# Loading the first memory head's cached keys inside the last differential head, both key products ahead of the sample scores, and memory queries made as 1, 2, 1 and 0 per head

## The chip, the cores and the metric

The kernel runs on one core of one Trainium2 chip. The core has a matrix engine (TensorE, PE in the profile; PEld is its weight load), a vector engine (VectorE, DVE), an activation engine (ScalarE, ACT), a general engine (GpSimd, POOL) and a queue engine (SyncE, SP) that issues nearly all transfers; 16 DMA engines move the data. The engines run their own instruction streams and meet through semaphores. The metric is the device time of one execution in microseconds (us).

## The reference, cut to what matters

One inference step of one layer. A prompt (1 stream of 1024 rows) and 8 running streams of 16 rows each, 1152 rows in all, share all weights. Three branches are computed from the normed input `h` (a recurrence, a differential attention with 8 heads, a cross-attention to a memory with 4 heads), then merged, and a ConvFFN follows. The change touches the end of the second branch and all of the third:

```python
def _mem_kv(mem, g, w):
    B, M, _ = mem.shape
    kv = (_rmsnorm(mem, g) @ w).reshape(B, M, 2, MEM_HEADS, MEM_DH)
    return (jnp.transpose(kv[:, :, 0], (0, 2, 1, 3)), jnp.transpose(kv[:, :, 1], (0, 2, 1, 3)))

def _mem_attention(q, mk, mv):
    B, L, _ = q.shape
    q = q.reshape(B, L, MEM_HEADS, MEM_DH)
    logits = jnp.einsum('blhd,bhmd->bhlm', q, mk.astype(q.dtype)).astype(jnp.float32) * (MEM_DH ** -0.5)
    p = jax.nn.softmax(logits, axis=-1).astype(q.dtype)
    return jnp.einsum('bhlm,bhmd->blhd', p, mv.astype(q.dtype)).reshape(B, L, MEM_HEADS * MEM_DH)
```

The prompt attends to 256 memory rows whose keys and values are computed here (`_mem_kv`); each of the 8 streams attends to keys and values of its own, read from a cache (`cache_mem_k`, `cache_mem_v`: 8 streams x 4 heads x 256 x 256 values). A head is 256 wide, so a head's queries are two tiles of 128 columns: 8 query tiles, Q0 to Q7.

## The kernel before, in words

The program is a sequence of phases (`norm_phase`, `hgrn_phase`, `diff_phase`, `mem_phase`, `merge_phase`, `ffn_phase`). Each phase is one block: every engine gets its list of instructions in program order, and no engine starts the next block's list before all have ended this one's. Every fp32 product is made as three products of rounded parts: ACT rounds a weight tile (`round_w`, L114), POOL makes the rest (`rest_w`, L119), PE multiplies (high x high, high x low, low x high). A weight tile passes through one of two staging slots, so the load of the tile after next waits until POOL has made the rest of this one (`load_w`, L107). Results go to one of two PSUM groups in strict turn (the class `Results`, by a list of names); PE takes the next group when ACT or DVE has freed it, and ACT and DVE wait for the count `full`.

`diff_phase`: 8 heads in a loop. On PE, "riders" (L1446, 24 products each) make the next head's projections between the steps; in the last head they make Q0 to Q2. After the last head PE makes Q3 (`next_product`, L151 to L153), while ACT and DVE finish the head's gate and output. SP then stores both (`store_branch`, L1106: the gate when `gt_r` is there, the output when `y_r` is), waits until both stores have landed, and its list ends. `probs` (L1018) holds the turned cached keys for the sample scores SL0 and SL1 of the differential head and is not used after SL1.

`mem_phase`: 4 heads, written out. A head's steps on PE, by the names in `orders` (L1591):

- K0, K1: the head's memory keys, two products of 24 matmuls (`memory_keys`, L151 to L153), from weights KA and KB. ACT copies each to `mem_kt` (`key`, L1704), and behind each copy rounds one of the value weights VA, VB.
- SL: the sample scores (`sample_scores`, L1917) from the cached keys that DVE has turned into `mem_probs` and `mem_probs_t` (`cached_kt`, L1812: each half waits for its 16 key loads), and from `mem_query_blocks`. SL stands between K0 and K1; ACT's `sample_exp` stands between its copies of K0 and K1.
- S: the prompt's scores (`prompt_scores`, L1937), which need both K0 and K1 copied.
- V: turned sample weights, key rows and values (L1926, L1894, L1905 to L1907); OS, PT, OT, O0, O1: sample output, turned prompt weights, turned sample output, prompt output in two halves (L1950, L1959, L1977, L1989).
- Queries of the next head: in heads 0 and 1 two tiles each (QA, QB). The first rides in OT, O0 and O1 (`riders`, L1595; products L166 to L168); the second is made in two results of its own, X and Y. Heads 2 and 3 make none.

SP (L1607 on) loads at the start of the block the 32 pieces of the cached keys of head 0 (`load_k`, 64 KB each, runs of 128 bytes), then 8 pieces of cached values, then the weights VA and VB of head 0; then, for each head, the next head's keys between the weight loads.

Of the kernel before, what the change touches and what calls it, by code (L numbers as in the profile page):

```python
# [6 lines left out]
F32 = mybir.dt.float32  # L7
# [5 lines left out]
ds = bass.ds  # L13

P = 128
# [980 lines left out]
def diff_phase(g):  # L996
# [16 lines left out]
    g.mem_parts = g.nc.alloc_sbuf_tensor_at("mem_parts", [P, 2, KT, MEM], F32R, offset=at)  # L1013
    vr, ot, sq, gt, qn, kn = (g.sb(n, [P, ROWS], ctx=ctx) for n in (
        "diff_v_rows", "diff_out", "diff_squares", "diff_gate", "next_q", "next_k"))
    qq, kk = g.first_q, g.first_k
    kr = vt
    pb = g.sb("probs", [P, 4, ROWS], ctx=ctx)  # L1018
# [53 lines left out]
    with nc.Block() as block:  # L1072
        @block.sync
        def _(sp):
# [83 lines left out]
            g.load_w(sp, wk[1], first + 6, HEADS - 1, NW)  # L1158
            store_branch(HEADS - 1)
# [401 lines left out]

def mem_phase(g):
# [8 lines left out]
    kc, vc = (g.sb(n, [P, DEC_B, MT, MD], ctx=ctx) for n in ("cached_mem_k", "cached_mem_v"))  # L1571
# [9 lines left out]
    kc_in = [g.sem(f"cached_mem_k{n}_in") for n in range(2)]  # L1581
    vc_in, qp_r = g.sem("cached_mem_v_in"), g.sem("mem_query_blocks_ready")
    shift_r, probs_r, s_shift_r, s_exp_r, s_probs_r, out_mk, out_mv, out_y = (g.sem(n) for n in (
        "mem_shifted", "mem_probs_ready", "mem_sample_shifted", "mem_sample_exp", "mem_sample_probs_ready",
        "mem_k_out", "mem_v_out", "y2_out"))
# [4 lines left out]
    swapped = (g.w + W["VA0"]) % 2  # L1590
# [4 lines left out]
    riders = [{"OT": (0, 2), "O0": (0, 0), "O1": (0, 1), "Y": (1, 1)},  # L1595
              {"OT": (0, 2), "O0": (0, 0), "O1": (0, 1), "Y": (1, 1)}, {}, {}]
    pair = ((1, 2), (1, 0))
    BLOCK = 32
    KC_DMAS = DEC_B // 2 * (P // BLOCK)
    kts = [(pr, pt), (pr, pt), (pr, pt), (pr, pt)]  # L1600

    def turned_keys(i, n):
        return flat(kts[i][n][:])[:, 0:PT * MEM]

    with nc.Block() as block:  # L1605
        @block.sync
        def _(sp):  # L1607
            def wkv(v, n, i):

                w = g.x["w_mem_kv"][0].rearrange("(k p) n -> p k n", p=P)  # L1610
                return w[:, :, ds(i * MD + (v * D + n * P), P)]

            def load_k(i, streams):

                for b in streams:
                    blocks = g.x["cache_mem_k"][0, b, ds(i, 1)].rearrange("h (r j) (c n) -> r (h j c) n", r=BLOCK, c=2)
                    for q in range(P // BLOCK):
                        sp.dma_start(kc[q * BLOCK:(q + 1) * BLOCK, b].rearrange("r c (j n) -> r (c j) n", n=BLOCK),
                                     blocks[:, :, q * BLOCK:(q + 1) * BLOCK]).then_inc(kc_in[b // 4], 16)
# [12 lines left out]

            load_k(0, range(DEC_B))
            load_v(0)
            wb = g.x["w_branch"][0, 0].rearrange("(k p) n -> p k n", p=P)
            for i in range(MH):
                last = i == MH - 1
                views = [wkv(1, n ^ swapped, i) for n in range(2)]
                for n, name in enumerate(("VA", "VB")):
                    g.load_w(sp, views[n], W[f"{name}{i}"])  # L1640
                if i < 2:
                    following = [(g.w_in(W_MQ + 4 + 2 * i), W[f"QA{i}"]), (g.w_in(W_MQ + 5 + 2 * i), W[f"QB{i}"])]
                else:
                    following = []
                if last:
                    following += [(wb[:, :, 0:P], W["B0"]), (wb[:, :, P:2 * P], W["B1"])]
                else:
                    following += [(wkv(0, 0, i + 1), W[f"KA{i + 1}"]), (wkv(0, 1, i + 1), W[f"KB{i + 1}"])]
                if last:
                    sp.wait_ge(kt_r, MH * 2)  # L1650
                    for k in range(3):
                        load_y0(k)
                else:
                    sp.wait_ge(kt_r, i * 2 + 2)
                    load_k(i + 1, range(0, 3))
                g.load_w(sp, *following[0])
                if not last:
                    load_k(i + 1, range(3, 4))
                g.load_w(sp, *following[1])
                if not last:  # L1660
                    load_k(i + 1, range(4, DEC_B))
                for view, j in following[2:]:
                    g.load_w(sp, view, j)
                if last:
                    for k in range(3, KT):
                        load_y0(k)
                else:
                    sp.wait_ge(g.full, R.full_value(f"OS{i}", 0))
                    load_v(i + 1)

        @block.scalar
        def _(act):
# [15 lines left out]
            def head(i):  # L1688
                last = i == MH - 1

                def query(t, c, ps, bank):
                    return act.activation(queries[i % 2][t][:, c * CW:(c + 1) * CW], ps[:, bank, 0:CW], ACT.Copy,
                                          scale=MD ** -0.5)
# [60 lines left out]
                if i < 2:  # L1754
                    g.round_w(act, W[f"QA{i}"])
                elif not last:
                    g.round_w(act, W[f"KA{i + 1}"])
                else:
                    g.round_w(act, W["B0"])
# [3 lines left out]
                if i < 2:  # L1763
                    g.round_w(act, W[f"QB{i}"])
                elif last:
                    g.round_w(act, W["B1"])
# [17 lines left out]
                if i < 2:  # L1784
                    g.round_w(act, W[f"KA{i + 1}"])
                    ps = ready("X")
                    for n, (t, c) in enumerate(pair):
                        ins = query(t, c, ps, 2 + n)
                    R.freed(ins, f"X{i}")
                if not last:  # L1790
                    if i == 1:
                        R.wait_freed(act, "X0")
                    elif i == 2:
                        R.wait_freed(act, "X1")
                    else:
                        R.wait_freed(act, "Q3")
                    sample_queries(i + 1)
                if i < 2:
                    ready("Y")
                    finish("Y", None)  # L1800
                if not last:
                    g.round_w(act, W[f"KB{i + 1}"])
# [4 lines left out]
        def _(dve):  # L1807
# [4 lines left out]
            def cached_kt(n, i):  # L1812
                dve.wait_ge(kc_in[n], 16 * KC_DMAS * (i + 1))
                if i:
                    dve.wait_ge(g.full, R.full_value(f"{('PT', 'O1')[n]}{i - 1}", 0))
                dve.transpose(turned_keys(i, n), kc[:, 4 * n:4 * n + 4].rearrange("p b c n -> p (b c n)"))\
                    .then_inc(kt_r, 1)
# [6 lines left out]
            def head(i):  # L1824
# [8 lines left out]
                def sample_normalize():  # L1833
                    dve.wait_ge(s_exp_r, i + 1)
# [38 lines left out]
        def _(pe):  # L1873
            pe.wait_ge(*g.mem_lo)

            def head(i):
                def query(ps, bank, t, c):
                    return g.gemm_piece(pe, ps[:, bank, 0:CW], g.w_parts(pe, W[f"{('QA', 'QB')[t]}{i}"]),
                                        (g.hhi, g.hlo), c)
# [30 lines left out]
                def sample_scores(ps):  # L1910
                    pe.wait_ge(qp_r, 2 * i + 2)
                    pe.wait_ge(kt_r, i * 2 + 2)
                    for n in range(2):
                        v = turned_keys(i, n).rearrange("p (b j c r) -> p b c j r", b=4, c=2, r=BLOCK)
# [77 lines left out]
                if i < 2:  # L1992
                    ps, _ = take("X")
                    for n, (t, c) in enumerate(pair):
                        ins = query(ps, 2 + n, t, c)
                    ins.then_inc(g.full, 1)
                    take("Y")[1].then_inc(g.full, 1)
# [856 lines left out]
```

## Time and profile before

| | |
|---|---|
| median of 3 runs | 3225.68 us (3223.38 to 3234.97) |
| the profiled execution | 3224.12 us |
| its span, first to last instruction | 3222.3 us |
| PE busy | 3103.0 us, 96% of the span |
| mean granted clock of PE | 0.983 of full speed |
| `mem_phase` in the span | from 1685.0 to 1908.5 us |
| PE's longest single wait in the whole span | 23.1 us, at 1688.1 us |

The profiled execution is 1.56 us below the median. A stretch is read by what PE waits for in it: the profile names for each idle time of PE the instruction that ended it. Times in the text are microseconds from the start of the span.

### The profile page before, as it was taken

The page shows a single profiled execution, that of the slowest core. Times are in us where ns is not written, and L with a number is a line of the kernel's source. Part 1 is how long each engine was busy: PE and PEld are TensorE (multiplying, and loading weights), DVE is VectorE, ACT ScalarE, POOL GpSimd, SP SyncE. Part 2 cuts the span into 40 slices and gives each one's busy share as a digit, 9 for nine tenths or more (in the row PEclk, how much of TensorE's full clock was granted, in tenths as well). Part 3 has the DMA queues.
Part 4 walks back from the last instruction along what each step waited for, and adds up shares of the span by engine and source line. Part 5 has one row for each costly group of instructions (what it writes and reads, how often), then busy time and mean ns, then how long its engine had stood idle before and what let it go on. Part 6 is the DMA issues. An engine that isn't in the chain of part 4 may idle for free. (4 is left out here: it accounts for less than half of the span.)

```text
span 3222.3 us, 49700 instructions
## 1 busy us (share of the span) xinstructions
PE 3103.0 (96%) x19550; PEld 2925.6 (91%) x19550; DVE 1369.2 (42%) x1448; ACT 1133.7 (35%) x1656; POOL 864.7 (27%) x524
## 2 busy tenths in 40 slices
PE   7899999999999999999997989999999999999997
PEld 6899999999988888888885879999999999999996
DVE  5554455443535555554542232132054444444443
ACT  5244433433334444544442342022242222222222
POOL 2333233322312112111121222343332322223320
PEclk8999999999999999999998999999999999999998
DMA  6312122121248768778856582432221111111101
GB/s 174 89 42 74 55 61 65 44 75 55 62 109 147 115 139 159 133 145 156 158 106 165 139 273 91 150 103 65 60 73 40 40 45 39 39 39 39 50 15 71
DMA packets 687891, 297.81 MB, mean 92 GB/s; under 512 B 350589, under 2 KB 668573, under 8 KB 687817
## 3 DMA queue, kind: packets, MB, share of 16 engines
q1 hardware_dynamic: 683368, 288.00, 37.4%
q10 hardware_dynamic: 4448, 8.80, 0.8%
q8 instruction: 50, 0.82, 0.1%
q14 instruction: 25, 0.20, 0.0%
HBM read 241.27 MB, written 55.46 MB: 92 GB/s over the span
## 5 line engine op out<-in xcount | busy, mean ns | idle before, releaser
L119 POOL TENSOR_TENSOR weight_lo<-weight_stage,weight_hi 128x1024 fp32r<-128x1024 f32 x180 | 449.9, 2500 | 1268.7 <-ACT weight_hi L114 1268.7
L2020 PE MATMUL group<-h_hi_part,weight_hi 128*128 128x384 f32 x1056 | 359.5, 340 | 6.3 <-DVE h_lo_part L2250 4.7
L2021 PE MATMUL group<-h_lo_part,weight_hi 128*128 128x384 f32 x1056 | 359.2, 340 | 0.0
L2022 PE MATMUL group<-h_hi_part,weight_lo 128*128 128x384 f32 x1056 | 359.1, 340 | 0.0
L114 ACT ACTIVATE weight_hi<-weight_stage 128x1024 fp32r<-128x1024 f32 x180 | 191.0, 1061 | 433.9 <-PE group L2287 241.2
L166 PE MATMUL group<-h_hi_part,weight_hi 128*128 128x384 f32 x912 | 324.0, 355 | 15.7 <-DVE key_rows L764 5.3
L167 PE MATMUL group<-h_lo_part,weight_hi 128*128 128x384 f32 x912 | 310.2, 340 | 0.0
L168 PE MATMUL group<-h_hi_part,weight_lo 128*128 128x384 f32 x912 | 310.1, 340 | 0.0
L1446 PE MATMUL group<-h_hi_part,weight_hi 128*128 128x384 f32 x768 | 268.2, 349 | 1.2 <-ACT next_v L1192 1.0
L1446 PE MATMUL group<-h_hi_part,weight_lo 128*128 128x384 f32 x768 | 261.5, 340 | 0.0
L2285 PE MATMUL group<-h_hi_part,weight_hi 128*128 128x384 f32 x768 | 259.2, 338 | 2.2 <-PEq L1605 2.2
L1446 PE MATMUL group<-h_lo_part,weight_hi 128*128 128x384 f32 x768 | 259.2, 338 | 0.0
L2286 PE MATMUL group<-h_lo_part,weight_hi 128*128 128x384 f32 x768 | 258.4, 337 | 0.0
L2287 PE MATMUL group<-h_hi_part,weight_lo 128*128 128x384 f32 x768 | 258.4, 336 | 0.0
L762 DVE COPY_PREDICATED scores<-level_masks,group 128x1152 f32<-128x1152 uint32 (+2 forms) x88 | 92.2, 1078 | 274.7 <-PE group L900 146.1
L2020 PEld LDWEIGHTS group<-h_hi_part,weight_hi 128*128 128x128 f32 x1056 | 199.3, 189 | 7.0 <-issue 5.4
L2021 PEld LDWEIGHTS group<-h_lo_part,weight_hi 128*128 128x128 f32 x1056 | 199.3, 189 | 0.0
L2022 PEld LDWEIGHTS group<-h_hi_part,weight_lo 128*128 128x128 f32 x1056 | 199.3, 189 | 0.0
L166 PEld LDWEIGHTS group<-h_hi_part,weight_hi 128*128 128x128 f32 x912 | 174.6, 191 | 25.2 <-issue 6.2
L167 PEld LDWEIGHTS group<-h_lo_part,weight_hi 128*128 128x128 f32 x912 | 174.7, 192 | 3.8 <-issue 2.9
L2576 DVE TENSOR_TENSOR residual<-residual,group 128x1152 f32<-128x1152 f32 x80 | 108.4, 1354 | 163.3 <-PE group L2691 163.3
L168 PEld LDWEIGHTS group<-h_hi_part,weight_lo 128*128 128x128 f32 x912 | 174.4, 191 | 0.0
(363 smaller groups left out, 6591.5 us busy)
## 6 DMA issues: line engine op xcount, KB each, us to landing
weight_stage<-in_w_in SPq DMA_DIRECT2D x88, 512.0 KB, 4.7
cached_v<-in_cache_diff_v SPq DMA_DIRECT2D x128, 256.0 KB, 5.1
cached_k<-in_cache_diff_k SPq DMA_DIRECT2D x224, 128.0 KB, 4.2
weight_stage<-in_w_up SPq DMA_DIRECT2D x44, 512.0 KB, 3.8
gate_in<-scratch_gates SPq DMA_DIRECT2D x24, 576.0 KB, 3.7
weight_stage<-in_w_branch SPq DMA_DIRECT2D x24, 512.0 KB, 4.0
down_stage<-in_w_down SPq DMA_DIRECT2D x22, 512.0 KB, 3.5
scratch_gates<-gate SPq DMA_DIRECT2D x16, 576.0 KB, 3.9
```

What stands on the lines that cost most here:

```text
L114: act.activation(self.whi[:, n % 2, :], self.wst[:, n % 2, :], ACT.Copy).then_inc(self.w_hi, 1)
L119: pool.tensor_tensor(self.wlo[:, n % 2, :], self.wst[:, n % 2, :], self.whi[:, n % 2, :].bitcast(F32), ALU.subtract).then_inc(self.w_lo, 1)
L166: pe.matmul(out, wh[:, k, :], xh[:, k, cols], start=(k == 0), stop=False)
L167: pe.matmul(out, wh[:, k, :], xl[:, k, cols], start=False, stop=False)
L168: last = pe.matmul(out, wl[:, k, :], xh[:, k, cols], start=False, stop=(k == KT - 1))
L1446: ins = pe.matmul(rider_bank, w[:, k, :], x[:, k, c * CW:(c + 1) * CW], start=(at == 0), stop=(at == STEPS - 1))
L2020: pe.matmul(o, w[0][:, k, :], ahi[:, k, rows], start=(k == 0), stop=False)
L2021: pe.matmul(o, w[0][:, k, :], alo[:, k, rows], start=False, stop=False)
L2022: last = pe.matmul(o, w[1][:, k, :], ahi[:, k, rows], start=False, stop=(k == KT - 1))
L2285: pe.matmul(o, wh[:, k, :], ahi[:, k, cols], start=(k == 0 and open_sum), stop=False)
L2286: pe.matmul(o, wh[:, k, :], alo[:, k, cols], start=False, stop=False)
L2287: last = pe.matmul(o, wl[:, k, :], ahi[:, k, cols], start=False, stop=(k == KT - 1))
```

## The change

Four things are done together.

- The buffer of the cached memory keys is placed on `probs`, and the 32 key loads of memory head 0 move from the start of `mem_phase` into the last differential head: on SP behind the last weight load and a wait for SL1, ahead of `store_branch`. `mem_phase` then starts with the value loads.
- In each memory head the order is K0 K1 SL instead of K0 SL K1. On ACT `sample_exp` moves behind both key copies and both roundings of value weights, and it frees the SL result itself (a separate semaphore goes).
- The queries are made as Q4 in head 0 (as a rider), Q5 (rider) and Q6 (in X and Y) in head 1, and Q7 in head 2 (rider). Before, head 0 made Q4 and Q5, head 1 made Q6 and Q7.
- The weight roundings on ACT follow: the tile behind VB is rounded after V, the next after OS, and in heads 0, 1 and 2 the third after O1. So in heads 0 and 2 the next head's KA is rounded after OS and its KB after O1.

```diff
@@ diff_phase
+    qq, kk = g.first_q, g.first_k
+    kr = vt
+    at = -(-g.nc.sbuf_base // 32) * 32
+    pb = g.sb("probs", [P, 4, ROWS], ctx=g.carried)
+    g.mem_kc = g.nc.alloc_sbuf_tensor_at("cached_mem_k", [P, DEC_B, MEM // P, MD], F32, offset=at)
...
             g.load_w(sp, wk[1], first + 6, HEADS - 1, NW)
+            sp.wait_ge(g.full, R.full_value("SL1", HEADS - 1))
+            load_mem_k(g, sp, 0, range(DEC_B))
             store_branch(HEADS - 1)
             sp.wait_ge(out_y, HEADS * 16 + 16)
             sp.wait_ge(out_gt, HEADS * 16 + 16)
@@ mem_phase
+    made = ((4,), (5, 6), (7,), ())
     W = {name: n for n, name in enumerate(
-        ["Q3"] + [f"{what}{i}" for i in range(MH)
-                  for what in ("KA", "KB", "VA", "VB") + (("QA", "QB") if i < 2 else ())] + ["B0", "B1"])}
+        ["Q3"] + [name for i in range(MH)
+                  for name in [f"{what}{i}" for what in ("KA", "KB", "VA", "VB")] + [f"Q{q}" for q in made[i]]]
+        + ["B0", "B1"])}
-    orders = ("K0 SL K1 S V OS PT OT O0 O1 X Y", "K0 SL K1 S V OS PT OT O0 O1 X Y",
-              "K0 SL K1 S V OS PT OT O0 O1", "K0 SL K1 S V OS PT OT O0 O1")
+    orders = ["K0 K1 SL S V OS PT OT O0 O1" + (" X Y" if len(made[i]) > 1 else "") for i in range(MH)]
...
-            load_k(0, range(DEC_B))
             load_v(0)
...
@@ mem_phase, ACT
                 key(0)
+                key(1)
                 ps = ready("SL")
-                ins = sample_exp(ps)
-                ins.then_inc(s_exp_r, 1)
-                act.wait_ge(s_exp_r, i + 1)
-                act.sem_inc(g.free[(R.base + R.k[f"SL{i}"]) % 2], 1)
-                key(1)
+                R.freed(sample_exp(ps), f"SL{i}")
...
                 act.dma_start(g.s["y_branch"][2, ds(i * 2, 2)].rearrange("a p n -> p a n"), yc[:]).then_inc(out_y, 16)
-                if i < 2:
-                    g.round_w(act, W[f"KA{i + 1}"])
+                if not last:
+                    g.round_w(act, W[f"VB{i}"] + 3)
+                if len(made[i]) > 1:
                     ps = ready("X")
...
@@ mem_phase, PE
                 memory_keys(0)
+                memory_keys(1)
                 ps, _ = take("SL")
                 sample_scores(ps).then_inc(g.full, 1)
-                memory_keys(1)
                 prompt_scores()
```

How the instructions stand, first on SP, from the last transfers of `diff_phase` to the first of `mem_phase` (the two branches are the end of the one block and the start of the next), before:

```order
L1157 DMA cached_k<-scratch_y_branch 128x8x256
L108 DMA weight_stage<-in_w_mem_kv 128x8x128
L1108 DMA scratch_gates<-diff_gate 128x1152
L1110 DMA scratch_y_branch<-diff_out 128x1152
L1072 UNCONDITIONAL_BRANCH
L1606 UNCONDITIONAL_BRANCH
L1618 DMA cached_mem_k<-in_cache_mem_k 32x16x32 x32
L1623 DMA cached_mem_v<-in_cache_mem_v 128x2x256 x8
```

and with the change:

```order
L1160 DMA cached_k<-scratch_y_branch 128x8x256
L108 DMA weight_stage<-in_w_mem_kv 128x8x128
L1574 DMA cached_mem_k<-in_cache_mem_k 32x16x32 x32
L1111 DMA scratch_gates<-diff_gate 128x1152
L1113 DMA scratch_y_branch<-diff_out 128x1152
L1075 UNCONDITIONAL_BRANCH
L1622 UNCONDITIONAL_BRANCH
L1631 DMA cached_mem_v<-in_cache_mem_v 128x2x256 x8
```

The 32 key loads now stand ahead of the two stores for which SP's list waits at its end. Second on ACT, memory head 0 from its first copy of keys (`mem_kt`) to the exponentials of the prompt, before:

```order
L1706 ACTIVATE mem_kt<-group 128x256
L114 ACTIVATE weight_hi<-weight_stage 128x1024
L1711 ACT_TABLE_LOAD
L1711 ACTIVATE sample_probs<-group 128x2x8x32
L1706 ACTIVATE mem_kt<-group 128x256
L114 ACTIVATE weight_hi<-weight_stage 128x1024
L1719 ACTIVATE mem_probs,mem_row_sum<-group,mem_row_max 128x256 x8
```

and with the change:

```order
L1710 ACTIVATE mem_kt<-group 128x256
L114 ACTIVATE weight_hi<-weight_stage 128x1024
L1710 ACTIVATE mem_kt<-group 128x256
L114 ACTIVATE weight_hi<-weight_stage 128x1024
L1715 ACT_TABLE_LOAD
L1715 ACTIVATE sample_probs<-group 128x2x8x32
L1723 ACTIVATE mem_probs,mem_row_sum<-group,mem_row_max 128x256 x8
```

The rounding of VA (the first L114) still stands between the two key copies; the sample exponential no longer does. Third on ACT, from the second half of head 0's prompt output to head 1's first copy of keys, before (`diff_q`, `diff_k`, `next_v` and `mem_q` hold queries):

```order
L1778 ACTIVATE mem_out<-group 128x1024
L1692 ACTIVATE diff_q<-group 128x384
L1783 DMA scratch_y_branch<-mem_out 128x2x1152
L114 ACTIVATE weight_hi<-weight_stage 128x1024
L1692 ACTIVATE diff_k<-group 128x384 x2
L1679 ACTIVATE mem_query_blocks<-next_v 128x8x16
L1679 ACTIVATE mem_query_blocks<-mem_q 128x8x16
L1692 ACTIVATE diff_k<-group 128x384
L114 ACTIVATE weight_hi<-weight_stage 128x1024
L1706 ACTIVATE mem_kt<-group 128x256
```

and with the change:

```order
L1771 ACTIVATE mem_out<-group 128x1024
L1696 ACTIVATE diff_q<-group 128x384
L1776 DMA scratch_y_branch<-mem_out 128x2x1152
L114 ACTIVATE weight_hi<-weight_stage 128x1024
L1683 ACTIVATE mem_query_blocks<-next_v 128x8x16
L1683 ACTIVATE mem_query_blocks<-mem_q 128x8x16
L1710 ACTIVATE mem_kt<-group 128x256
```

Before, the first L114 there rounds KA of head 1 and the second KB, with the evictions of X and Y between; now the only one rounds KB, and head 1's first key copy follows at once.

## Rows read from the trace of the kernel before

**Rows 1.** PE's waits in mem_phase: us in total, times, longest

```profile
PE group L1917 <- DVE mem_probs_t L1816: 23.1, 1, 23.1
PE group L1937 <- ACT mem_kt L1706: 4.7, 3, 3.6
...
PE group L2285 <- PEq L1605: 2.2, 1, 2.2
```

**Rows 2.** Timeline of SP, 1600 to 1725: start us, us, line, transfer, [idle before]

```profile
1653.55 5.80 SPq L1103 DMA_DIRECT2D cached_v<-in_cache_diff_v  x8
...
1660.21 1.66 SPq L108 DMA_DIRECT2D weight_stage<-in_w_mem_kv  x1
1678.16 0.36 SPq L1108 DMA_DIRECT2D scratch_gates<-diff_gate  x1
1678.57 0.43 SPq L1110 DMA_DIRECT2D scratch_y_branch<-diff_out  x1
1684.83 21.47 SPq L1618 DMA_DIRECT2D cached_mem_k<-in_cache_mem_k  x32
1706.34 4.20 SPq L1623 DMA_DIRECT2D cached_mem_v<-in_cache_mem_v  x8
...
1713.31 11.66 SPq L1618 DMA_DIRECT2D cached_mem_k<-in_cache_mem_k  x12
```

**Rows 3.** DMA instructions of L1618 by stretch: duration ns min/median/max, first and last start

```profile
L1618 SPq DMA_DIRECT2D cached_mem_k<-in_cache_mem_k x32: 610/627/719, 1684.8 to 1705.7; - x32
...
L1618 SPq DMA_DIRECT2D cached_mem_k<-in_cache_mem_k x2: 1401/2161/2921, 1713.3 to 1716.3; - x2
```

**Rows 4.** SP's own wait, 1676 to 1690, and the output store's landing

```profile
SPq L1072 <- PEq L1072: 2.2, 1, 2.2
...
DMA to landing us min/median/max: 3.9/3.9/3.9
```

**Rows 5.** Timeline of ACT and DVE in memory head 0

```profile
1718.05 1.06 ACT L114 ACTIVATE weight_hi<-weight_stage 128x1024 fp32r<-128x1024 f32 x1 [29.52 <-DMA weight_stage<-in_w_mem_kv]
1721.64 0.38 ACT L1706 ACTIVATE mem_kt<-group 128x256 f32<-128x256 f32 x1
...
1697.54 2.31 DVE L1816 STREAM_TRANSPOSE mem_probs<-cached_mem_k 128x2048 f32<-128x2048 f32 x1 [12.04 <-DMA cached_mem_k<-in_cache_mem_k]
```

**Rows 6.** Timeline of PE: end of diff_phase, prompt scores of heads 0 to 3

```profile
1684.07 0.34 PE L153 MATMUL group<-h_hi_part,weight_lo 128*128 128x384 f32 x1
1722.17 0.67 PE L1937 MATMUL group<-mem_kt,diff_q 128*128 128x256 f32 x2 [3.56 <-ACT mem_kt L1706]
1783.02 0.67 PE L1937 MATMUL group<-mem_kt,next_v 128*128 128x256 f32 x2 [0.52 <-issue]
1842.25 0.67 PE L1937 MATMUL group<-mem_kt,diff_q 128*128 128x256 f32 x2 [0.56 <-ACT mem_kt L1706]
1878.97 0.67 PE L1937 MATMUL group<-mem_kt,next_v 128*128 128x256 f32 x2 [0.56 <-ACT mem_kt L1706]
```

**Rows 7.** Ends of prompt output (PE), and POOL's rests of KB, heads 0 to 2

```profile
1758.71 3.60 PE L1989 MATMUL group<-mem_probs_t,mem_v_rows 128*128 128x512 f32 x8
1862.65 7.10 PE L1989 MATMUL group<-mem_probs_t,mem_v_rows 128*128 128x512 f32 x16 [1.62 <-ACT mem_probs_t L1738]
...
1765.34 2.39 POOL L119 TENSOR_TENSOR weight_lo<-weight_stage,weight_hi 128x1024 fp32r<-128x1024 f32 x1 [20.35 <-ACT weight_hi L114]
1835.52 2.38 POOL L119 TENSOR_TENSOR weight_lo<-weight_stage,weight_hi 128x1024 fp32r<-128x1024 f32 x1 [8.61 <-ACT weight_hi L114]
```

**Rows 8.** Stretches: busy us (x), then PE's granted clock, DMA share, GB/s

```profile
1774.60:1777.50 2.90, 2.90 (x26) 2.83 (x24) 0.00 (x0) 1.44 (x2) 1.16 (x1) 1.00 0.00 0
1777.50:1779.50 2.00, 2.00 (x35) 1.01 (x33) 0.00 (x0) 1.33 (x2) 1.65 (x2) 1.00 0.00 0
1723.20:1726.60 3.40, 3.40 (x10) 2.69 (x9) 0.00 (x0) 0.00 (x0) 2.19 (x1) 0.50 0.64 103
1908.70:1912.10 3.40, 3.40 (x20) 3.40 (x21) 0.00 (x0) 0.00 (x0) 0.00 (x0) 1.00 0.98 315
```

More of the change, by code:

```diff
@@ L1559, in diff_phase, with load_mem_k @@
     ctx.close()
+MEM_BLOCK = 32
+def load_mem_k(g, sp, i, streams):
+    for b in streams:
+        blocks = g.x["cache_mem_k"][0, b, i:i + 1].rearrange("h (r j) (c n) -> r (h j c) n", r=MEM_BLOCK, c=2)
+        for q in range(P // MEM_BLOCK):
+            sp.dma_start(g.mem_kc[q * MEM_BLOCK:(q + 1) * MEM_BLOCK, b].rearrange("r c (j n) -> r (c j) n", n=MEM_BLOCK),
+                         blocks[:, :, q * MEM_BLOCK:(q + 1) * MEM_BLOCK]).then_inc(g.mem_kc_in[b // 4], 16)
 def mem_phase(g):
@@ L1570, in mem_phase @@
     pr, pt = (g.sb(n, [P, PT, MEM], ctx=ctx) for n in ("mem_probs", "mem_probs_t"))
-    kc, vc = (g.sb(n, [P, DEC_B, MT, MD], ctx=ctx) for n in ("cached_mem_k", "cached_mem_v"))
+    kc, vc = g.mem_kc, g.sb("cached_mem_v", [P, DEC_B, MT, MD], ctx=ctx)
     mhi, mlo = g.mem_parts[:, 0], g.mem_parts[:, 1]
@@ L1637, in _ @@
                 last = i == MH - 1
-                views = [wkv(1, n ^ swapped, i) for n in range(2)]
+                views = [wkv(1, n ^ swapped[i], i) for n in range(2)]
                 for n, name in enumerate(("VA", "VB")):
                     g.load_w(sp, views[n], W[f"{name}{i}"])
-                if i < 2:
-                    following = [(g.w_in(W_MQ + 4 + 2 * i), W[f"QA{i}"]), (g.w_in(W_MQ + 5 + 2 * i), W[f"QB{i}"])]
-                else:
-                    following = []
+                following = [(g.w_in(W_MQ + q), W[f"Q{q}"]) for q in made[i]]
                 if last:
@@ L1689, in head, with query @@
                 last = i == MH - 1
-                def query(t, c, ps, bank):
-                    return act.activation(queries[i % 2][t][:, c * CW:(c + 1) * CW], ps[:, bank, 0:CW], ACT.Copy,
-                                          scale=MD ** -0.5)
+                def query(q, c, ps, bank):
+                    return act.activation(queries[q // 2 % 2][q % 2][:, c * CW:(c + 1) * CW], ps[:, bank, 0:CW],
+                                          ACT.Copy, scale=MD ** -0.5)
                 def ready(n):
@@ L1753, in head @@
                 finish("V", rows_out(ps))
-                if i < 2:
-                    g.round_w(act, W[f"QA{i}"])
-                elif not last:
-                    g.round_w(act, W[f"KA{i + 1}"])
-                else:
-                    g.round_w(act, W["B0"])
+                g.round_w(act, W[f"VB{i}"] + 1)
                 store_rows("V")
@@ L1762, in head @@
                 finish("OS", act.activation(ps_s[:], ps[:, 0:2, 0:MD], ACT.Copy))
[L1763 to L1766, printed above, removed]
+                g.round_w(act, W[f"VB{i}"] + 2)
                 probs_turned()
@@ L1783, in head @@
                 act.dma_start(g.s["y_branch"][2, ds(i * 2, 2)].rearrange("a p n -> p a n"), yc[:]).then_inc(out_y, 16)
-                if i < 2:
-                    g.round_w(act, W[f"KA{i + 1}"])
+                if not last:
+                    g.round_w(act, W[f"VB{i}"] + 3)
+                if len(made[i]) > 1:
                     ps = ready("X")
-                    for n, (t, c) in enumerate(pair):
-                        ins = query(t, c, ps, 2 + n)
+                    for n, (q, c) in enumerate(pair):
+                        ins = query(q, c, ps, 2 + n)
                     R.freed(ins, f"X{i}")
                 if not last:
-                    if i == 1:
-                        R.wait_freed(act, "X0")
-                    elif i == 2:
+                    R.wait_freed(act, "Q3" if i == 0 else f"OT{i}")
+                    if i == 2:
                         R.wait_freed(act, "X1")
-                    else:
-                        R.wait_freed(act, "Q3")
                     sample_queries(i + 1)
-                if i < 2:
+                if len(made[i]) > 1:
                     ready("Y")
                     finish("Y", None)
-                if not last:
                     g.round_w(act, W[f"KB{i + 1}"])
@@ L1991, in head @@
                     ins.then_inc(g.full, 1)
-                if i < 2:
+                if len(made[i]) > 1:
                     ps, _ = take("X")
-                    for n, (t, c) in enumerate(pair):
-                        ins = query(ps, 2 + n, t, c)
+                    for n, (q, c) in enumerate(pair):
+                        ins = query(ps, 2 + n, q, c)
                     ins.then_inc(g.full, 1)
```

48 lines of the change are left out of this document (19 added, 29 removed).

## The prediction, made before the changed kernel ran

> **What bounds the kernel now.** I read PE's waits first. In `mem_phase` one wait stands out: 23.1 us, ended by DVE's second turned half of the cached keys; the only other one of size is 4.7 us in three pieces, of which 3.6 us ended with a copy of memory keys on ACT [rows 1]. SP's timeline says why the first is so long: the 32 key loads start only with the block, at 1684.83, and are issued in 21.47 us [rows 2], 627 ns each [rows 3]. DVE turns the first half at 1697.54 after waiting for its loads, 2.31 us of work [rows 5]; PE had its first key product and then nothing. Behind the keys SP issues 8 value loads, and behind these the value weights. VA is rounded on ACT at 1718.05, after 29.52 us of waiting for that load [rows 5]: 11.7 us after the first value load was issued at 1706.34 [rows 2]. The copy of K1 stands behind this rounding in ACT's list, and PE's prompt scores of head 0 start at 1722.17 behind the copy [rows 6]. So there are two chains in a row, the keys and then the value weights, and the change takes only the first out of the block.
>
> **Where the key loads go.** On SP they come behind the last weight load, which ended at 1661.87 [rows 2]; there SP had been idle until the gate was ready at 1678.16, 16.3 us. In a free queue 32 loads take 21.47 us. Here the queue isn't free: 8 value loads of 2 MB, 1 MB of memory rows and a weight tile of 0.5 MB were issued from 1653.55 on. The nearest row is the 12 key loads at 1713.31, which stand behind 2 MB of values and two weight tiles, 7 us after the first of these, and take 11.66 us instead of 12 x 0.67 = 8.0 [rows 2]; the first two alone take 2.92 and 1.40 [rows 3]. I take 11.66 for the first 12 and 20 x 0.67 = 13.4 for the others: the burst ends at 1661.87 + 25.1 = 1686.9. Lower bound: no slowing, 1683.3. Upper bound: all 32 at 11.66 / 12 = 0.97, 1693.0.
>
> By the Trainium skill (Perfetto Trace Analysis, What "DMA-bound" means) an issuing queue that is solid with transfer instructions is bound by making descriptors, and their window holds no movement of data. Read strictly, the burst would cost 32 x 0.627 = 20.1 us whatever is queued ahead, end at 1682.0, and the sum below would be 3204.2 us. The 2921 ns of the row are against it, so I keep 25.1.
>
> **What that delays.** The gate's store was issued at 1678.16 and the output's at 1678.57, and SP was done before PE: it waited 2.2 us for PE at the block's end [rows 4]. Now the gate store is issued at 1686.9 and the output's at 1687.35, and the latter lands 3.9 us later [rows 4], at 1691.25. PE's last product of `diff_phase` ends at 1684.07 + 0.34 = 1684.41 and SP's next block began 0.4 us later, at 1684.83 [rows 2, 6]. So SP is now the last to arrive, and the new block begins at 1691.25 + 0.4 = 1691.65: 6.8 us later than before. All engines wait for that.
>
> **The start of the new block.** SP issues the values at once and VA behind them: 11.7 us as before, so VA has landed at 1703.35. DVE turns both halves, 2 x 2.31 us [rows 5], within the first 5.5 us. PE makes K0 in 2.9 us [rows 8]; the rest of KB is there after ACT's 1.06 [rows 5] and POOL's 2.39 [rows 7], so K1 runs from some 3.7 to 6.6 us into the block and SL (1.9 of the 2.0 us in [rows 8]) to 8.5. PE then waits for ACT: rounding VA 1.06, copying K1 0.38 [rows 5], 0.15 to PE. Prompt scores of head 0 start at 1703.35 + 1.6 = 1704.95 instead of 1722.17: **-17.2 us**. Not the 23.1 us of the wait: 6.8 go to the late block, and the value weights' chain is uncovered in place of the keys'. VB's rounding, `sample_exp` and what follows it on DVE run while PE makes the prompt scores; I cost them at nothing under that cover.
>
> **Later heads.** With SL behind K1, K1 must wait for the rest of KB with only K0 as cover.
> - Head 0 to 1. O1 ends at 1758.71 + 3.60 = 1762.31 on PE; the tile that ACT rounds there has its rest at 1765.34 + 2.39 = 1767.73 [rows 7], 5.4 us later. That slot is KB's now. K0 covers 2.9; K1 starts at +5.6, SL at +8.5, the scores at +10.4. Before, they started at 1783.02 [rows 6], of which X and Y were 12.3 (1762.31 to 1774.6): +8.4. **+2.0 us.**
> - Head 1 to 2. X and Y stay; the rest of KB is there at 1835.52 + 2.38 = 1837.90 [rows 7], so the scores start at 1837.90 + 0.2 + 2.9 + 1.9 = 1842.9 instead of 1842.25 [rows 6]: **+0.6.**
> - Head 2 to 3. O1 ends at 1862.65 + 7.10 = 1869.75 [rows 7]; before, the scores came 9.2 us behind it [rows 6], now 10.4: **+1.2.**
> - The rider of Q7 in head 2's OT covers the wait for the turned prompt weights, 1.62 us [rows 7]: **-1.6.**
>
> X and Y of head 0 are made as riders of head 2, the same products in all: nothing. SP's other loads keep their places in the heads, and their distance to the rounding changes by no more than these terms of 2 us, so they have no term of their own.
>
> **The sum.** -17.2 + 2.0 + 0.6 + 1.2 - 1.6 = -15.0 us. Against the profiled execution, 1.56 us below the median: 3224.12 - 15.0 = 3209.1 us, 0.5% below the median of 3225.68. About 0.5% (16.1 us, 3209.6) is what a measurement of this kernel can tell from no change, so the forecast stands right at that bound.
>
> **The clock.** After the 3.56 us wait at 1722.17 [rows 6] PE ran at half its clock (1.2 of 2.4 GHz) from 1723.20 to 1726.60; after the 2.2 us at the end of `mem_phase` [rows 1], at 1908.70, it stayed at full [rows 8]. A stretch of 3.4 us at half costs 1.7. The new wait ahead of head 0's prompt scores is some 3 to 4.5 us, like the old one, so I leave that cost as it is, and give it 1.7 either way. The two new waits of 2.7 us (heads 0 to 1, 2 to 3) lie between the two rows; I take no fall for them, 3.4 us for both as the upper bound. The Trainium skill (TensorE: Matmul & The Clock Gate, HAM oscillation) says that waits between bursts of products can make each burst start at the low clock; by it, if both waits are long enough, the time would be 3212.5.
>
> **Rivals.**
> 1. *More is given back (chance 0.27).* The burst goes at 0.97 us throughout, or the new waits for KB cost the clock too: +6.1 and +3.4 at most, 3212 to 3218.6. For it: 2.92 us for a single load behind a full queue. Against: two of the 12 loads account for 3.0 of the 3.6 us of slowing.
> 2. *The burst is hidden better and VA comes sooner (0.24).* No slowing (-3.6) and, with the values alone in the queue, VA landing up to 1.5 us earlier; no fall of the clock ahead of the scores (-1.7): 3202.3 at the least. For it: 627 ns in a free queue.
> 3. *Slower (0.03).* The stores behind the burst: each us by which the burst ends later starts the block a us later. The gain is gone when it takes 25.1 + 15.0 = 40.1 us, 1.25 us per load, and 0.5% is lost at 1.76. The second load behind the full queue took 1.40; if all did, the burst would take 44.8 us and the time would be 3228.8. Against it: 20 of the 32 come after the backlog.
> 4. *The wait only changes its name (0.04).* If VA landed 11.7 + 15.0 = 26.7 us into the block, as late as the keys did, PE would wait there as long as before and nothing would be gained: 3224. Against it: the 11.7 us of the rows.
>
> **How the numbers follow.** The forecast, 3205 to 3212, has 0.42; a little over half of it lies below 3209.6. Rival 2 adds all of its 0.24 to faster: 0.24 + 0.24 = 0.48. Rivals 1 and 4 and the rest of the forecast are within 0.5%: 0.27 + 0.04 + 0.18 = 0.49. Slower by over 0.5%: 0.03. The range takes in the bounds of rivals 1 and 2 but for their ends: 3202 to 3217.
>
> **What would show it.** Right: SP's 32 key loads from 1662 to 1687, the first two far over 627 ns; PE's first product of the memory heads at 1692, ended by SP's queue and not by PE; no wait for `mem_probs_t`; 3 to 5 us ahead of head 0's prompt scores, ended by `mem_kt`, with ACT waiting for the weight load ahead of it; waits of 2.7, 1.3 and 2.7 us for `weight_lo` ahead of K1 in heads 1 to 3; one wait for `mem_probs_t` less. Wrong: a block that begins before 1689 or after 1695, VA rounded other than 11 to 12 us into the block, or half-clock stretches behind the waits for `weight_lo`.

## The result, and the profile after

The changed kernel takes 3209.43 us (median of 7 runs, 3206.96 to 3215.59) against 3227.87 us of the kernel before (7 runs, 3223.38 to 3234.97): a ratio of 0.9946, 95% interval 0.9934 to 0.9958, clear of 1. The profiled execution took 3207.9 us, its span 3206.1 us, 16.2 less than before.

PE's waits in the memory heads of the changed kernel (us in total, times, longest) answer to [rows 1]:

```profile
PE group L151 <- PEq L1075: 8.2, 1, 8.2
PE group L151 <- POOL weight_lo L119: 6.5, 3, 2.6
PE group L1926 <- ACT mem_kt L1710: 3.0, 1, 3.0
...
PE group L2274 <- PEq L1621: 2.2, 1, 2.2
PE group L1978 <- ACT mem_probs_t L1742: 1.6, 1, 1.6
```

The 23.1 us for the turned cached keys are gone. In their place stand 8.2 us at the block's start, 6.5 us in three pieces for the rest of a weight tile (KB ahead of K1 in heads 1 to 3), and 3.0 us ahead of head 0's prompt scores. SP's timeline from the end of `diff_phase` on answers to [rows 2]:

```profile
1659.53 1.62 SPq L108 DMA_DIRECT2D weight_stage<-in_w_mem_kv  x1
1661.20 25.80 SPq L1574 DMA_DIRECT2D cached_mem_k<-in_cache_mem_k  x32
1687.04 0.62 SPq L1111 DMA_DIRECT2D scratch_gates<-diff_gate  x1
1687.70 0.43 SPq L1113 DMA_DIRECT2D scratch_y_branch<-diff_out  x1
1692.00 3.98 SPq L1631 DMA_DIRECT2D cached_mem_v<-in_cache_mem_v  x8
1696.02 2.30 SPq L108 DMA_DIRECT2D weight_stage<-in_w_mem_kv  x2
```

The 32 key loads now end at 1687.00, the two stores are issued behind them, and the block begins at 1692.00. The loads by duration (ns, min/median/max), the first three and then all, answer to [rows 3]:

```profile
L1574 SPq DMA_DIRECT2D cached_mem_k<-in_cache_mem_k x3: 1187/1454/2219, 1661.2 to 1665.0; - x3
```

```profile
L1574 SPq DMA_DIRECT2D cached_mem_k<-in_cache_mem_k x32: 626/627/2219, 1661.2 to 1686.4; - x32
```

PE's timeline: the start of the block, the prompt scores of heads 0 to 3 (L1926, as in [rows 6]), the waits ahead of K1 (L151), and the end of the memory phase (L2274):

```profile
1692.19 0.55 PE L151 MATMUL group<-mem_parts,weight_hi 128*128 128x256 f32 x1 [8.15 <-PEq L1075]
...
1704.38 0.67 PE L1926 MATMUL group<-mem_kt,diff_q 128*128 128x256 f32 x2 [3.02 <-ACT mem_kt L1710]
...
1750.05 0.55 PE L151 MATMUL group<-mem_parts,weight_hi 128*128 128x256 f32 x1 [2.65 <-POOL weight_lo L119]
...
1756.41 0.70 PE L1926 MATMUL group<-mem_kt,next_v 128*128 128x256 f32 x2
...
1811.46 0.36 PE L151 MATMUL group<-mem_parts,weight_hi 128*128 128x256 f32 x1 [1.22 <-POOL weight_lo L119]
...
1816.34 0.70 PE L1926 MATMUL group<-mem_kt,diff_q 128*128 128x256 f32 x2
...
1860.36 0.36 PE L151 MATMUL group<-mem_parts,weight_hi 128*128 128x256 f32 x1 [2.65 <-POOL weight_lo L119]
...
1865.20 0.70 PE L1926 MATMUL group<-mem_kt,next_v 128*128 128x256 f32 x2
...
1894.96 0.41 PE L2274 MATMUL group<-h_hi_part,weight_hi 128*128 128x384 f32 x1 [2.23 <-PEq L1621]
```

The prompt scores of head 0 start 17.8 us sooner than before, the merge 13.7 us sooner (1894.96 against 1908.70, the start of the last stretch in [rows 8]). So some 4 us of the gain are given back inside the memory phase. ACT's timeline says what holds the first scores, as [rows 5] did:

```profile
1702.91 1.06 ACT L114 ACTIVATE weight_hi<-weight_stage 128x1024 fp32r<-128x1024 f32 x1 [5.81 <-DMA weight_stage<-in_w_mem_kv]
1703.87 0.36 ACT L1710 ACTIVATE mem_kt<-group 128x256 f32<-128x256 f32 x1
```

VA is rounded 10.9 us into the block, after waiting for its load, and the copy of K1 stands behind it. Last, the clock behind PE's waits (busy us of PE, PEld, DVE, ACT and POOL, then the granted clock, DMA share, GB/s): in K0 and K1 at the block's start, in the prompt scores of head 0, behind the 2.65 us ahead of head 1's K1, and behind the 2.65 us ahead of head 3's:

```profile
1692.20:1695.80 3.60, 3.60 (x18) 3.60 (x19) 3.60 (x3) 2.35 (x4) 2.39 (x1) 0.56 0.69 219
...
1706.10:1709.50 3.40, 3.40 (x11) 2.69 (x10) 0.50 (x1) 2.84 (x3) 2.64 (x2) 0.57 0.53 82
...
1750.50:1753.90 3.40, 3.40 (x20) 3.40 (x20) 0.00 (x0) 0.00 (x0) 1.74 (x1) 0.58 0.84 199
...
1860.40:1863.80 3.40, 3.40 (x33) 3.10 (x37) 0.00 (x0) 0.35 (x1) 2.16 (x1) 1.00 0.62 193
```

The second has its like in [rows 8]. The first is new, but the wait for VA covers it; the third is new and is not covered. Behind the last wait PE stays at full, though it is as long as the one before.

### The profile page after: what moved, and what is told of

Read it like the earlier page. It is cut to its first block and busy times, and to the rows that moved or that the text cites. A ratio compares the mean times of both kernels' runs of the same rounds, so it can differ in the third digit from the quotient of the medians.

```text
span 3206.1 us, 49696 instructions
## 1 busy us (share of the span) xinstructions
PE 3100.3 (97%) x19550; PEld 2923.5 (91%) x19550; DVE 1368.8 (43%) x1448; ACT 1132.8 (35%) x1656; POOL 864.5 (27%) x524
## 5 line engine op out<-in xcount | busy, mean ns | idle before, releaser
L114 ACT ACTIVATE weight_hi<-weight_stage 128x1024 fp32r<-128x1024 f32 x180 | 190.9, 1061 | 413.9 <-PE group L2276 241.2
L2274 PE MATMUL group<-h_hi_part,weight_hi 128*128 128x384 f32 x768 | 258.8, 337 | 2.2 <-PEq L1621 2.2
L166 PEld LDWEIGHTS group<-h_hi_part,weight_hi 128*128 128x128 f32 x912 | 174.2, 191 | 25.1 <-issue 6.2
```

Source lines behind the costliest of these rows:

```text
L114: act.activation(self.whi[:, n % 2, :], self.wst[:, n % 2, :], ACT.Copy).then_inc(self.w_hi, 1)
L166: pe.matmul(out, wh[:, k, :], xh[:, k, cols], start=(k == 0), stop=False)
L2274: pe.matmul(o, wh[:, k, :], ahi[:, k, cols], start=(k == 0 and open_sum), stop=False)
```

## The experiments

**How they are compared.** A kernel's whole time varies from run to run (that of the kernel before from 3221.2 to 3240.3 us in the first group of experiments), and what lies outside the changed stretch varies too: from the end of the memory phase to the end of the span the profiled executions of these kernels show 1310.5 to 1315.4 us. So beside each ratio stands the stretch in question, taken from PE's timeline of the profiled execution as differences of starts: the wait at the block's start; from the block's first product to head 0's first prompt scores; from there to head 3's; and, with head 3's own 29.7 to 30.1 us, the sum from the wait to the merge. These columns are one execution of each kernel and need not stand for its median. The ratios are to the kernel before, run beside each group of experiments on the same chip.

| kernel | wait at block start | to scores, head 0 | heads 0 to 3 | sum | ratio, 95% |
|---|---|---|---|---|---|
| before | 0.61 | 37.15 | 156.80 | 224.29 | 1 |
| after | 8.15 | 12.19 | 160.82 | 210.92 | 0.9946 [0.9934, 0.9958] |
| after, with the second group | 8.14 | 12.19 | 160.86 | 210.95 | 0.9940 [0.9921, 0.9959] |
| early keys alone | 8.15 | 15.05 | 157.48 | 210.41 | 0.9965 [0.9953, 0.9977] |
| order alone | 0.61 | 33.93 | 159.15 | 223.58 | 0.9990 [0.9979, 1.0002] |
| VA and VB first | 8.46 | 10.46 | 159.00 | 207.67 | 0.9934 [0.9914, 0.9954] |
| stores on ACT | 5.22 | 12.32 | 158.97 | 206.63 | 0.9921 [0.9901, 0.9941] |
| queries 2, 2, 0, 0 | 7.32 | 12.12 | 154.80 | 204.14 | 0.9936 [0.9916, 0.9955] |
| VA first, stores on ACT | 3.57 | 9.24 | 157.70 | 200.28 | 0.9932 [0.9913, 0.9951] |
| all three | 6.40 | 9.28 | 154.86 | 200.44 | 0.9921 [0.9902, 0.9939] |
| all three, again | 5.53 | 10.18 | 154.81 | 200.27 | 0.9908 [0.9889, 0.9927] |
| all three, two queues | 2.77 | 9.22 | 156.72 | 198.46 | 0.9904 [0.9888, 0.9921] |

**1. Early keys alone.** The kernel before with the first item of the change; order and queries stay.

```diff
@@ diff_phase, SP
             g.load_w(sp, wk[1], first + 6, HEADS - 1, NW)
+            sp.wait_ge(g.full, R.full_value("SL1", HEADS - 1))
+            load_mem_k(g, sp, 0, range(DEC_B))
             store_branch(HEADS - 1)
...
@@ mem_phase, SP
-            load_k(0, range(DEC_B))
             load_v(0)
```

> One part alone: the kernel before with only the early key loads; order K0 SL K1 and queries 2, 2, 0, 0 as before. Theory (the early loads carry the whole gain, order and queries together give a little back): the new block starts at 1692.0 as with the full change and VA is rounded 10.9 us later; sample_exp with its table load (2.4 us) again stands ahead of the copy of K1, so the prompt scores of head 0 start 2.6 us later than with the full change, at 1707.0; from there to the end of mem_phase 186.5 us as before, against 190.6 with the full change. Net 1.5 us faster than the full change: about 16 to 19 us below the kernel before. Rival (order and queries carry a good part of the gain): 10 us or less below the kernel before.

Measured: 3217.91 us, 0.9965. ACT's timeline in head 0:

```profile
1704.26 1.06 ACT L114 ACTIVATE weight_hi<-weight_stage 128x1024 fp32r<-128x1024 f32 x1 [5.06 <-DMA weight_stage<-in_w_mem_kv]
1705.33 1.28 ACT L1721 ACT_TABLE_LOAD   x1
1706.62 1.10 ACT L1721 ACTIVATE sample_probs<-group 128x512 f32<-128x512 f32 x1
1707.84 0.38 ACT L1716 ACTIVATE mem_kt<-group 128x256 f32<-128x256 f32 x1
```

The old order leaves the table load and the sample exponential between VA's rounding and K1's copy, and head 0's scores come 15.05 us into the block instead of 12.19: the new order is worth 2.9 us there. But heads 0 to 3 take 3.3 us less than in the changed kernel, so that the whole stretch is no longer (210.4 against 210.9 us). In the trace the key loads alone carry the gain, 13.9 of 224.3 us. The runs do not bear this out in full: the median is 12.4 us below the kernel before, between the theory's 16 to 19 and the rival's 10, and the two intervals only just overlap. The profiled execution, 3209.23 us, is the fastest of ten (the others 3212.64 to 3226.64). Where those lose their time no trace shows, so it stays open whether order and queries add to the gain.

**2. Order alone.** The kernel before with K0 K1 SL on PE and ACT; keys, queries and the other roundings as before.

```diff
@@ mem_phase, PE
                 memory_keys(0)
+                memory_keys(1)
                 ps, _ = take("SL")
                 sample_scores(ps).then_inc(g.full, 1)
-                memory_keys(1)
...
```

> One part alone: the kernel before with only the order K0 K1 SL (and sample_exp behind both key copies); key loads and queries as before. Theory: the 23 us wait for the turned keys stays; prompt scores of head 0 start 2.5 us earlier, since the copy of K1 no longer stands behind sample_exp; the three later heads give back 0.7, 0.7 and 1.1 in waits for the rest of KB: within 1 us of the kernel before. Rival (the order is part of the gain): 4 us or more faster.

Measured: 3226.49 us, 0.9990: nothing that can be told. PE's waits:

```profile
PE group L1914 <- DVE mem_probs_t L1813: 19.9, 1, 19.9
PE group L151 <- POOL weight_lo L119: 5.6, 4, 2.7
PE group L1934 <- ACT mem_kt L1706: 3.8, 1, 3.8
```

K1 moved under the wait for the cached keys takes 3.2 us off it, and the waits for KB give most of that back. Without the early keys the order has little to gain.

**3. VA and VB ahead of the values.** The changed kernel; SP issues head 0's value weights first in the block, then the cached values.

```diff
@@ mem_phase, SP
-            load_v(0)
...
                 for n, name in enumerate(("VA", "VB")):
                     g.load_w(sp, views[n], W[f"{name}{i}"])
+                if i == 0:
+                    load_v(0)
```

> The full change, and in mem_phase the two value weight loads of head 0 go ahead of the 8 value loads. Theory (ACT's wait for VA sets the start of the prompt scores): VA is rounded some 5 us after the block's start instead of 10.9, no wait for mem_kt is left, prompt scores start right behind SL, 3.0 us earlier; the half-clock stretch in them may go too, another 1.7: 3 to 5 us faster than the full change. Rival (the sample scores or PE's own work set it): same start within 0.5 us.

Measured: 3207.74 us, 0.9934. PE's waits in the memory heads:

```profile
PE group L151 <- PEq L1075: 8.5, 1, 8.5
PE group L151 <- POOL weight_lo L119: 6.5, 3, 2.6
PE group L1940 <- issue: 2.9, 4, 0.7
```

The wait for `mem_kt` is gone altogether: it was the value weights' place in SP's queue. The scores start 1.7 us sooner in the block; the rest of the 3.0 us is lost to PE itself, which runs K0 and much of K1 at half its clock behind the 8.5 us at the block's start (granted 0.50 from 1695.20 to 1698.60 and 0.58 from 1698.60 to 1702.00), with nothing left to hide it. Heads 0 to 3 take 1.8 us less, as the prompt scores of head 0 stay at full here, and the sum falls by 3.3 us, as expected. The interval overlaps that of the changed kernel.

**4. The last stores on ACT's queue.** The changed kernel; gate and output of the last differential head are stored by ACT, as soon as they are ready, not by SP behind the key loads.

```diff
@@ diff_phase, SP
             load_mem_k(g, sp, 0, range(DEC_B))
-            store_branch(HEADS - 1)
@@ diff_phase, ACT, last head
+                    act.wait_ge(gt_r, i + 1)
+                    act.dma_start(g.s["gates"][ds(i + 16, 1)].rearrange("a p n -> p (a n)"), gt[:]).then_inc(out_gt, 16)
+                    act.wait_ge(y_r, i + 2)
+                    act.dma_start(g.s["y_branch"][1, ds(i, 1)].rearrange("a p n -> p (a n)"), ot[:]).then_inc(out_y, 16)
                     act.wait_ge(hmem_in, 16)
```

> The full change, and the last head's two stores are issued from ACT's queue, so that they no longer stand behind the 32 key loads on SP. Theory (the stores behind the burst make the block late): they land before the burst's end, the block starts when SP has issued the burst, at 1687.4 instead of 1692.0, and the time falls by 4 to 5 us against the full change. Rival (the landing of the keys or the burst itself holds the block's end in another way, or the stores land as late from ACT's queue): block start moves by less than 1 us.

Measured: 3205.2 us, 0.9921. SP's timeline:

```profile
1663.34 27.02 SPq L1577 DMA_DIRECT2D cached_mem_k<-in_cache_mem_k  x32
1691.01 1.42 SPq L1634 DMA_DIRECT2D cached_mem_v<-in_cache_mem_v  x3
```

The block begins 0.65 us behind the last key load's issue, where it was 5.0 us behind it. PE's wait falls only from 8.2 to 5.2 us, because in this execution the loads took 1.2 us longer: now their issue alone ends last. The clock in head 0's prompt scores, at full here, gives another 1.9 us in heads 0 to 3. The interval overlaps that of the changed kernel.

**5. Queries made as before.** The changed kernel with Q4 and Q5 in head 0, Q6 and Q7 in head 1; the weight roundings on ACT move with them.

```diff
@@ mem_phase
-    made = ((4,), (5, 6), (7,), ())
+    made = ((4, 5), (6, 7), (), ())
...
-    pair = ((6, 2), (6, 0))
+    pair = [((q[1], 2), (q[1], 0)) if len(q) > 1 else () for q in made]
...
```

> The changed kernel, but the queries are made as before: Q4 and Q5 in head 0, Q6 and Q7 in head 1, none in head 2; the new key placement and the new order K0 K1 SL stay. Theory A (the move of the queries gives nothing here, because X and Y of head 0 are what covers the rest of KB1): the 2.65 us wait for weight_lo ahead of head 1's K1 falls to about 1.2 us or less and the half-clock stretch behind it goes (1.7 us more), the 2.65 us wait in head 2 to 3 goes too since KA3 is rounded behind V and KB3 behind OS; against that a second wait of 1.62 us for the turned prompt weights comes back in head 2. Net -2 to -5 us of the changed kernel: 3204.5 to 3207.5. Theory B (riding pays: the query products in head 2 fill waits that are idle otherwise): +1 to +3 us, 3210.5 to 3212.5.

and, beside it, the changed kernel itself:

> The changed kernel itself, unaltered, on the same chip as the three variants: 3207 to 3212 us by either theory, 0.994 to 0.996 of the kernel before. It is the number that the variants of this call are compared with.

Measured: 3206.68 us, 0.9936, against 3210.18 us, 0.9940. The intervals overlap; the traces differ clearly, by 6.8 us in the stretch. PE's waits with the old queries:

```profile
PE group L151 <- PEq L1075: 7.3, 1, 7.3
PE group L1976 <- ACT mem_probs_t L1742: 3.2, 2, 1.6
PE group L1937 <- issue: 2.9, 4, 0.7
PE group L151 <- POOL weight_lo L119: 2.4, 2, 1.2
```

Two waits of 1.22 us for KB are left of 2.65, 1.22 and 2.65, and the second wait for the turned prompt weights is back: 6.5 - 2.4 = 4.1 us won, 1.6 lost. The rest of the 6.8 us is not the queries' work alone: 0.8 is a shorter wait at the block's start, and the clock adds to it, as the prompt scores run at full here (granted clock in the third last column):

```profile
1704.40:1707.80 3.40, 3.40 (x16) 3.01 (x17) 0.00 (x0) 2.70 (x3) 3.40 (x2) 1.00 0.83 109
1707.80:1711.20 3.40, 3.40 (x18) 2.99 (x17) 1.54 (x3) 0.75 (x1) 0.93 (x1) 1.00 0.59 98
```

X and Y of head 0 had stood between O1 and K0 and covered the rest of KB; as riders of head 2 they cover a wait of 1.6 us instead. In the trace theory A holds and theory B falls: the move of the queries costs time.

**6. Edits 3 and 4 together.**

> The changed kernel with the last head's two stores issued from ACT's queue and VA and VB of memory head 0 loaded ahead of the cached values. Theory A (late block and late VA are two terms of a sum): each gain adds, -2.9 us at the wait for SP's queue and -3.0 to -3.6 at the wait for mem_kt, together -5 to -7 us: 3202.5 to 3204.5. Theory B (they share one chain, the DMA traffic behind the burst: with the block sooner, VA lands later in it): only the larger of the two, 3205.5 to 3206.5.

Measured: 3205.34 us, 0.9932: between the two theories' times, so the runs do not decide. The profiled execution, 3200.23 us, is the fastest of six, its stretch 10.7 us shorter than in the changed kernel beside it. In this trace the gains add, and more: the wait at the start fell by 4.6 us, the way to the scores by 3.0, and heads 0 to 3 by 3.2, because the half-clock stretches in head 0's prompt scores and behind the wait ahead of head 1's K1 were not there. Behind that wait, 2.65 us as before:

```profile
1743.90:1747.30 3.40, 3.40 (x36) 3.10 (x40) 0.00 (x0) 0.37 (x1) 2.11 (x1) 1.00 0.68 175
```

**7. All three edits (3, 4 and 5), twice.**

> Both loads and stores changed as in the run before, and the queries made as 2, 2, 0, 0. Theory A (three separate terms): another -2 to -5 us, 3198 to 3202. Theory B (the queries' move pays): 3204 to 3207, slower than the run with 1, 2, 1, 0.

> The run with all three edits again, unaltered, on the same chip as the run with two queues: 3201 to 3206 us by either theory; PE's wait at the block's start between 3.5 and 6.5 us, as the burst takes 26 to 28 us.

Measured: 3203.66 us, 0.9921, and, with the next experiment, 3199.68 us, 0.9908. The first median lies between the theories, the second below the range expected of it. Heads 0 to 3 take 154.9 and 154.8 us, 2.8 and 2.9 less than in 6: the queries' price with the clock left out. In the first of the two the gain went again at the start, where the burst of keys took 28.40 us instead of 25.97 and PE waited 6.4 us instead of 3.6.

**8. Two queues.** As 7, but the last 8 of the 32 early key loads are issued by ACT's queue.

```diff
@@ diff_phase, SP
-            load_mem_k(g, sp, 0, range(DEC_B))
+            load_mem_k(g, sp, 0, range(6))
@@ diff_phase, ACT, last head
                     g.round_w(act, first + 5, i, NW)
+                    act.wait_ge(g.full, R.full_value("SL1", HEADS - 1))
+                    load_mem_k(g, act, 0, range(6, DEC_B))
```

> As the run with all three edits (stores on ACT's queue, VA and VB ahead of the values, queries 2, 2, 0, 0), and of the 32 early key loads the last 8 (two of the eight streams) are issued by ACT's queue, behind ACT's last rounding of the differential phase, instead of SP's. Theory A (what makes the block late is the time SP's queue takes to issue the loads, some 0.6 us each behind the backlog): SP ends 8 x 0.63 = 5 us sooner, ACT issues its 8 in about 5 us from some 1684 on, and PE's wait at the block's start falls from 3.6 to 6.4 us to 2 to 3 us: 2 to 4 us less, 3199.5 to 3202. Theory B (the loads are held up by the DMA engines' backlog, whichever queue issues them): the wait stays at 3.5 to 6.5 us and the time at 3202 to 3205.5.

Measured: 3199.51 us, 0.9904, against 3199.68 us of the run with one queue beside it: by the times no difference. The queues' timelines, SP's and ACT's, and PE's wait:

```profile
1663.97 20.88 SPq L1579 DMA_DIRECT2D cached_mem_k<-in_cache_mem_k  x24
1688.55 4.01 SPq L108 DMA_DIRECT2D weight_stage<-in_w_mem_kv  x2
```

```profile
1680.97 2.62 ACTq L1579 DMA_DIRECT2D cached_mem_k<-in_cache_mem_k  x2
...
1683.62 4.26 ACTq L1579 DMA_DIRECT2D cached_mem_k<-in_cache_mem_k  x6
```

```profile
PE group L151 <- PEq L1075: 2.8, 1, 2.8
```

SP's burst ends at 1684.85 and ACT's at 1687.88, and the block begins at 1688.55. PE's wait is 2.8 us, against 3.6 to 6.4 in the three executions with stores on ACT, VA first and one queue for the keys, as theory A has it: issuing sets the block's start. By the Trainium skill (Perfetto Trace Analysis, DMA Optimizations), where generating descriptors is the bottleneck, balancing the transfers over several issuing engines may help; the trace agrees, with 2.8 us instead of the 5.5 of the run beside it. Heads 0 to 3 took 1.9 us more in this execution, all of it in head 2 to 3 (PE's granted clock 0.69 and 0.81 in its prompt output), so that the sum gained only 1.8 us, below what the runs can tell.

## Why the prediction was right, point by point

- *The burst.* Predicted 1661.87 to 1686.9; measured 1661.20 to 1687.00, 25.8 us instead of 25.1. That most of the slowing falls on the first loads holds: the first three (2219, 1454 and 1187 ns) account for 3.0 of the 25.8 - 21.5 = 4.3 us, one later load (1662 ns) for 1.0; the median over all is 627 ns. The strict reading of the Trainium skill (Perfetto Trace Analysis, What "DMA-bound" means), 20.1 us, does not agree with the 25.8 us, and the measurement decides.
- *The late block.* Predicted 1691.65, measured 1692.00. Experiment 4 shows the cause: with the stores out of the way, the block begins 0.65 us behind the burst.
- *Head 0's scores.* Predicted 1704.95, 17.2 us sooner; measured 1704.38, 17.8. VA was rounded 10.9 us into the block, predicted 11.7. So it fell just outside the 11 to 12 us that the prediction had set as a sign of being wrong. Experiment 3 shows that the place of its load was the cause of the wait. One thing the prediction left out: behind the 8.2 us at the block's start PE ran at half its clock (0.56 over 3.6 us), and SL ended 9.4 us into the block instead of 8.5. The wait for VA covered it, 3.0 us of wait being left.
- *Later heads.* The three waits for KB were predicted at 2.7, 1.3 and 2.7 us and measured 2.65, 1.22 and 2.65. Head 1 to 2 cost 59.93 - 59.23 = +0.7 (predicted +0.6). Head 2 to 3 took 48.86 us; against 36.72 before and 12.3 for the rider's products that is -0.2 (predicted 1.2 - 1.6 = -0.4).
- *The term that was mis-sized* is head 0 to 1: predicted +2.0 us; measured 52.03 - (60.85 - 12.3) = +3.5. The step that failed is "I take no fall for them": behind one of the two 2.65 us waits PE ran at half its clock (0.58), as rival 1 had it for both. Experiments 3 and 6 price it: head 0 to 1 took 50.20 us with this half-clock stretch and 48.88 without, 1.3 of the 1.5 us. The prediction's own sign for this error, half-clock stretches behind the waits for `weight_lo`, was there.
- *The sum.* In the memory phase -17.8 + 3.5 + 0.7 - 0.2 = -13.8 us, where -15.0 had been predicted (the merge starts 13.7 sooner); in the second profiled execution the stretch is 224.29 - 210.95 = 13.3 us shorter. The other 2.4 of the 16.2 us lie behind the memory phase, which the change does not touch; the second execution has 0.9 there. The forecast took its 15.0 us off a profiled execution of 3224.12 us, 3.8 below the later median of the kernel before; the medians differ by 18.4 us, of which the stretch shows 13.4. That the median came within 0.4 us of the forecast is in part luck.
- *Rivals.* Of rival 1 only the clock came, and half of it. Rivals 3 and 4 fell with the burst's 25.8 us and VA's 10.9 us. Rival 2's sooner VA came by 0.8 us.

What the prediction did not ask is what each of the four items is worth. In the profiled executions, in the stretch: the early keys -13.9 us (experiment 1); order and roundings on top of them 204.14 - 210.41 = -6.3 (of which 0.8 is the wait at the start, 2.9 the way to head 0's scores, and the rest in heads 0 to 3, where the clock differs too); the queries 210.95 - 204.14 = +6.8, of which 0.8 is again the wait at the start, and 2.9 is left with the clock left out (experiment 7). In these traces the last two about cancel, and the change gives what its first item alone gives. The medians show the first item, 12.4 us against 18.4 for the whole change, but don't confirm the rest: the kernel of experiment 5 is 3.5 us below the changed one with overlapping intervals, and experiment 1's profiled execution is the fastest of its ten. The best kernels of the study, with the stores on ACT, VA first and the queries left as they were, take 3199.5 to 3203.7 us, 0.9904 to 0.9921 of the kernel before.

## What to carry to other kernels

Loads moved ahead into another block are priced by what stands behind them in their queue: here the loads end 3.0 us behind PE's last product, and two stores behind them, for whose landing the block's end waits, cost 5.0 us more; another queue for the stores mends it. When a wait is removed, read what was queued behind it (the value weights) and order those loads by who needs them first. A piece of work that looks free to move may be the cover of another chain: ask what waits in the place that it leaves, not only what it fills in the place it goes to.

## What the runs showed of the hardware

- Behind waits of one length the clock did not behave alike. After 2.65 us ahead of head 1's K1, PE fell to half in four executions (changed kernel twice, experiments 3 and 4: granted 0.56 to 0.60 in the stretch behind) and stayed at full in experiment 6 (1.00); after the same 2.65 us ahead of head 3's K1 it stayed at full in all five. Waits of 1.22 us were followed by full clock wherever they were looked at.
- The prompt scores of head 0 ran partly at half behind waits of 3.02 and 2.93 us (0.57 and 0.54) and at full behind 2.48 and 2.08 us (1.00). But a wait of 1.89 us, ahead of head 2's prompt output in experiment 8, was followed by 0.69 and 0.81. At the block's start PE ran at half behind every wait from 2.8 to 8.5 us (0.50 to 0.62 over the first 3.4 to 3.6 us).
- Most of the 64 KB loads in runs of 128 bytes kept their queue 627 ns, behind a backlog too; the first three took up to 2.2 us in the changed kernel, one later load 1.66 us. The burst of 32 took 24.8 to 28.4 us in these kernels. Why its longest cases come with the stores on ACT's queue was not tried.
